# Samples' attention: twelve of a quad's sixteen pages asked for by GpSimd, four and all unpaged quads by SyncE

## What is computed

```python
# branch A, selected blocks: keys and values come through a page table
phys = page_table[b_ix, jp // BLOCKS_PER_PAGE]
past_kv = cache_sel[phys[..., None], layer, rows, :, g_ix[..., None], :]
o_sel = gathered_attention(q, sel_kv[..., 0, :], sel_kv[..., 1, :], kpos, ok, qpos)
# branch A, sliding window of 512 rows, from a contiguous cache
sw = einsum('bsgrd,bkgd->bsgrk', q, win_ext[:, :, 0]) * ATTN_SCALE
# branch B, dilated attention: three head groups, from contiguous caches
s = einsum('bshd,bsnhd->bshn', q, kvg[:, :, :, 0]) * ATTN_SCALE
```

## Time and profile before

| | us |
|---|---|
| median of three runs | 1706.0 |
| lowest and highest | 1697.8, 1709.15 |
| the profiled execution, own time | 1713.18 |
| its span, first to last instruction | 1711.5 |

### The profile page before, as it was taken

One profiled execution on the slowest core, in us unless ns is written; L12 is line 12 of the kernel. 1 busy time (PEld: TensorE's weight loads), 2 busy tenths in 40 slices (PEclk: granted clock), 3 DMA queues, 4 the chain that ended last, 5 costly groups with the idle time before them and its releaser, 6 DMA issues. The chain is left out here.

```text
span 1711.5 us, 25862 instructions
## 1 busy us (share of the span) xinstructions
PE 1591.7 (93%) x9452; PEld 1257.3 (73%) x9452; DVE 807.6 (47%) x1757; ACT 306.7 (18%) x830; POOL 191.8 (11%) x333
## 2 busy tenths in 40 slices
PE   8999999999799999998588887889989999999997
PEld 3787888899688887776345555568878888888885
DVE  3532666676545456566513210024667666632334
ACT  2220144434402122324011321100010000000000
POOL 0001300000000000100265564400000000000000
PEclk9999999999899999999699999899999999999999
DMA  9997443444399988823599997955221222222221
GB/s 304 355 339 258 123 129 103 120 121 126 110 344 325 376 309 327 294 77 109 191 326 318 327 315 264 335 207 190 75 74 60 88 75 85 88 74 84 89 74 52
DMA packets 188975, 326.90 MB, mean 191 GB/s; under 512 B 21105, under 2 KB 123058, under 8 KB 187954
## 3 DMA queue, kind: packets, MB, share of 16 engines
q1 hardware_dynamic: 157138, 182.76, 32.5%
q0 software_dynamic: 27104, 129.65, 21.4%
q10 hardware_dynamic: 4608, 12.85, 2.2%
HBM read 307.71 MB, written 109.32 MB: 244 GB/s over the span
## 5 line engine op out<-in xcount | busy, mean ns | idle before, releaser
L1610 PE MATMUL bank<-hT,wring 128*128 128x272 f32 x704 | 181.6, 400 | 1.9 <-PEq L1301 1.2
L2205 POOL DMA_DIRECT2D ring<-in_sel_pages x256 | 139.5, 545 | 227.8 <-issue 163.0
L1610 PEld LDWEIGHTS bank<-hT,wring 128*128 128x128 f32 x704 | 131.0, 192 | 31.6 <-issue 4.6
L2590 PEld LDWEIGHTS bank<-hT,xk 128*128 128x128 f32 x512 | 102.1, 205 | 53.9 <-issue 32.2
L2590 PE MATMUL bank<-hT,xk 128*128 128x272 f32 x512 | 136.7, 423 | 0.0
L2843 PE MATMUL bank<-hT,wring 128*128 128x272 f32 x392 | 95.4, 392 | 0.0
L1032 PEld LDWEIGHTS bank<-wring,w 128*128 128x128 f32 x768 | 89.5, 194 | 8.0 <-issue 7.5
L1032 PE MATMUL bank<-wring,w 128*128 128x128 f32 x768 | 94.3, 279 | 0.0
L2843 PE MATMUL bank<-aT,wring 128*128 128x272 f32 x352 | 85.9, 392 | 0.0
L2843 PEld LDWEIGHTS bank<-hT,wring 128*128 128x128 f32 x392 | 74.5, 190 | 15.4
L324 POOL DMA_DIRECT2D out_new_dil<-in_cache_dil x24 | 15.1, 634 | 559.0 <-DMA out_new_dil<-in_cache_dil 267.9
(11 more groups left out here) (414 smaller groups left out, 2700.2 us busy)
## 6 DMA issues: line engine op xcount, KB each, us to landing
wring<-in_w SPq DMA_DIRECT2D x147, 512.0 KB, 4.5
out_new_dil<-in_cache_dil POOLq DMA_DIRECT2D x8, 8176.0 KB, 46.4
wring<-in_cmp_pages SPq DMA_DIRECT2D x128, 128.0 KB, 2.3
ring<-in_sel_pages POOLq DMA_DIRECT2D x256, 64.0 KB, 4.4
ring<-in_sel_pages SPq DMA_DIRECT2D x256, 64.0 KB, 4.3
out_new_dil<-in_cache_dil POOLq DMA_DIRECT2D x8, 2032.0 KB, 15.1
ring<-in_dil_k SPq DMA_DIRECT2D x9, 1024.0 KB, 8.0
ring<-in_dil_k POOLq DMA_DIRECT2D x9, 1024.0 KB, 6.6
```

The source lines that it names most:

```text
L1610: mm = pe.matmul(product_bank(p, n), w[:, P * k:P * k + P], HH[x][:, k, :], start=(k == 0), stop=(k == 3))
L2205: eng.dma_start(slot[:, j, P * i:P * i + P], t["sel_pages"][bass.ds(page, 1), :, P * kv:P * kv + P].rearrange("o p n -> (o p) n")).then_in ...
L2590: mm = pe.matmul(gate_bank(h), gw[u % 2][:, P * k:P * k + P], hT[:, k, HT * hf:HT * hf + HT], start=(k == 0), stop=(k == KD - 1))
```

## The change

Of a paged quad SyncE now issues the four pages of sample 0, and GpSimd the twelve of samples 1, 2 and 3. All unpaged quads are SyncE's. The counts that TensorE waits for follow. No instruction of the other engines changes, nor the order of the quads, the ring or the bytes.

```diff
@@ quad_shares
             name = QUADS[n][0]
             if name in ("sel", "sel_v"):
-                return 8, 8
-            return (1, 0) if n % 4 < 2 else (0, 1)
+                return 4, 12
+            return 1, 0
@@ load_quad
             if name in ("sel", "sel_v"):
                 kv = int(name == "sel_v")
-                for j in (2 * who, 2 * who + 1):
+                for j in ((0,), (1, 2, 3))[who]:
                     pages = page_numbers(engine, (GB * gg + j) * PAGES + 4 * c, 4)
```

## The result

The changed kernel takes 1732.55 us (median of four runs, 1731.22 to 1734.86) against 1706.33 of before in the runs taken beside it. The ratio is 1.0171, with a 95% interval of 1.0143 to 1.0199: slower by 1.7%. The forecast was 1710 with a range of 1698 to 1728, so the time lies outside. The profiled execution took 1733.13 us, 20.0 more than that of before.

What follows compares the result with a forecast made beforehand. GpSimd's asking for pages, 8.07 to 8.16 us a pair, was to become the bound of the steady stretches. The walk's +3.5 us gave 1716.7 on the profile, 1709.5 against the median, say 1710; range 1706 - 8 to 1706 + 22.

Steps and rivals of the forecast that it cites:

- the walk: Follows GpSimd's asking and TensorE's reads through the samples' attention stage; its sum was +3.5 us, 1716.7 on the profiled execution.
- between the halves: Between the two halves of the values: 17.7 us from read to read, where it had been 23.5.
- eighth read of the first keys: TensorE's eighth read of paged quads in the first keys: forecast at 900.9 against 898.66 before, +2.2 us.
- the long run: Second keys and first values: sixteen paged quads, the sixteenth starting at 1031.4 with holds and read from 1042.0, +7.5 us.
- own time: The profiled execution's total: 1713.2 us before, forecast as 1716.7 after adding +3.5 us.
- Landing, taken as 3.5 us: Time from issue to landing of GpSimd's last page in a paged quad: 3.5 us, with ends 2.8 and 6.5.
- Holds, taken as 6.7 us in the long run and 1.3 after: Interruptions of GpSimd's asking: 6.7 us over second keys and first values (bounds 0 and 10), 1.3 in second values.
- the holds under VectorE's scaling: GpSimd's asking held during VectorE's scaling of probabilities: two holds of up to 2.16 us, 3.5 us together.
- Second keys and first values, one unbroken run of sixteen quads: The seam from keys to values keeps the ring's order; sixteenth quad starts 121.7 us after 903.0, before holds.
- So against the median I forecast 1709.5, say 1710: Whole kernel: the profiled execution lay 7 us above the median 1706.0, so 1716.7 was lowered to 1709.5.
- The slower rival: GpSimd's groups cost 3.0 us instead of 2.7 under unbroken use: 75 x 0.28 = 21 us more, +22, 1728; chance 0.22.
- transfers bound it: Rival: transfers set the stage's pace whoever asks, +0 us, 1706; decides where a pair needs over 8.07 us; chance 0.17.

Runs made afterwards that it cites:

- the dose by two: Against the changed kernel, GpSimd's page numbers are loaded two at a time instead of four: 1799.93 us, ratio 1.0568 to the kernel before.

## Why the prediction was wrong

Its mechanism was right: the asking of GpSimd became the bound, at the usual group steps that were worked out; TensorE waits for pages and no longer for dilated values; SyncE's side cost nothing and by itself gains 8 us. The chance it gave to a loss above 1% was 0.18, and its number was too small by 22.5 us. What failed are sizes in the sum: what GpSimd loses beside its clean groups (10.4 us more than the walk allowed), the landing of the last page (5.1 us more), and the 7 us taken off at the end. The first two and -0.2 between the halves are the 15.3 us by which the walk ended too early. By the steps of the walk:

| step | forecast | measured |
|---|---|---|
| third quad of the first keys asked for | 850 | 849.8 |
| eighth read of the first keys | 900.9 | 903.95 |
| sixteenth quad of the long run asked for | 1031.4 | 1038.6 |
| its read | 1042.0 | 1051.8 |
| from there to the second half's first read | 17.7 | 17.5 |
| eighth read of the second values | 1114.5 | 1129.8 |
| own time | 1716.7 | 1733.1 |

- *Landing, taken as 3.5 us.* From the last page's issue (1.71 us after its group) to the read it was 4.6, 5.5 and 5.5 us at the three places where it counts: 897.65 + 1.71 to 903.95; 1046.3 (the end of the twelve pages at 1038.55, less one page) to 1051.78; 1122.62 + 1.71 to 1129.84. That is 1.1 + 2.0 + 2.0 = 5.1 us. I had thinned out the queue in thought, but GpSimd's pages took 4.3 us to land in the median where they had taken 4.4, and the DMA engines stayed 0.84 to 0.92 busy, 0.92 in the first keys where 0.85 was expected.
- *Holds, taken as 6.7 us in the long run and 1.3 after.* The stops had 4.5 us of these 8.0. They took 2.63, 2.64 and 3.64 above the gap of 0.05 that is usual within a group, so 8.9. There were also gaps of about 1.4 us between groups, such as at 894.97, which the walk lacked. Against that the holds under VectorE's scaling, 3.5 us for two, were over-priced. The twelve pages at 1038.55 lie beside one and took 8.26 us, 0.5 more than 3 x 2.31 + 2 x 0.41, and the twenty at 968.22 lie beside the other and took 13.37, 0.4 more than 5 x 2.28 + 4 x 0.4. One page's DMA did take up to 2.5 us there. But the pages after it follow without the gap of 0.4 between groups, and most is made up. The Trainium skill's "SBUF — State Buffer", section "SBUF: two separate sides", says that GpSimd is shut out for the instruction's length. The single DMA agrees (2.50 and 2.16 us beside instructions of 2.4); the cost at the end of the run was 0.4 and 0.5 us.
- *"Second keys and first values, one unbroken run of sixteen quads".* The step missed that its second quad takes the slot of the window quad: GpSimd stood 2.10 us at 916.71 for the read of L2310. The run from 906.03 to 1038.55 took 132.5 us, 4.1 more than the 128.4 forecast; in the second values 1071.71 to 1117.18 is 45.5 us against 42.1. With everything in them these are 2.9 and 3.0 us a group.
- *"So against the median I forecast 1709.5, say 1710".* This step moved the whole profile down by the 7 us by which the old kernel's profiled execution lay above its median. But the new bound does not scatter with the old: the changed kernel's runs lie within 3.6 us, its profile within 0.6 of its median, while the runs of before lie between 1694.5 and 1712.5. The walk gave an absolute time, and that, 1716.7, should have stood; its upper end would then have been 1735. It is 7 of the 22.5 us missed; the walk's terms are 15.3 (3.1 to the eighth read, 6.7, -0.2 and 5.7 in the three parts after it), 1.1 lies behind the stage, and the remainder, -1.1, is my rounding and the 0.6 us by which the changed kernel's profile lay above its median.
- *The slower rival.* It came nearest with its 1728 and decides from a mean of 2.9 us a group on. That mean was reached, not because every group got slower, as it says, since most stayed at 2.68 to 2.72, but by stops and gaps. It put 25 quads on the chain; the dose by two gives 31. Its sum does not come out either: 21 us on the forecast without its 8.0 us of holds is +16.5, and on the whole forecast +24.5, not +22.

The rival "transfers bound it" failed at its own condition: the pair's bytes need less than 8.1 us, for the same bytes ran in 1695.6 us. The Trainium skill's "DMA: Bandwidth & Descriptors", section "Issuing engines are not separate DMA queues", calls the saved issue time usually small beside the transfer; here a page asked for in 0.67 us took 4.3 to land, so that agrees for one page. Added up over twelve of 64 KB on one engine, the issue time was the whole difference between 1695.6 and 1732.6.

## What to carry to other kernels

When DMAs of 64 KB are shared between issuing engines, price a tile per engine as instructions times start-to-start step, register loads included, and keep every engine's sum clearly below the pace of the consumer: here the time was nearly flat up to about 80% of the pace of 7.5 to 8 us, and rose by 19 and then by 31 us per microsecond beyond it. Take the price from the loaded stage and not from the first instructions of an empty queue, and see first that no wait for a slot hides in the row that it is read from. Where a change moves the bound to something steady, forecast the absolute time from the profile and don't carry over the distance between the old kernel's profile and its median.

## What the runs showed of the hardware

- GpSimd needed 0.53 us for a page DMA of 64 KB and 0.75 for one of 256 KB; with the page numbers loaded by four it was 0.67 us a page.
- A register load of two page numbers took 512 ns on GpSimd, one of four 319 ns.
- In the versions with twelve pages by GpSimd and all unpaged quads by SyncE, it stopped for 1.5 to 4.7 us after every 108 pages asked for, and after every 120 where one DMA brings four. The cause is open.
- Beside VectorE's scaling of 128x4100 numbers (2.4 us) one page DMA of GpSimd's took 2.2 to 2.5 us instead of 0.53; over the pages that follow all but 0.4 to 0.5 us was made up.
- SyncE asked for twelve pages in 7.9 us in the loaded stage, 0.66 us a page with its loads, so in numbers of pages it was no faster than GpSimd there.
